# Modulation held as columns, small and expert loads moved ahead, and 29 instead of 31 fixed rounds in the second expert layer

## The reference, cut to what matters

```python
mod = silu(c) @ w_ada + b_ada                       # one row of 6 * 1024
sh1, sc1, g1, sh2, sc2, g2 = split(mod, 6)
h = rms_norm(x, norm1_g) * (1 + sc1) + sh1
ca, cb, q, k, v, gate_conv, gate_attn = split(h @ w_in)
merged = sigmoid(gate_conv) * conformer_conv(ca, cb) + sigmoid(gate_attn) * diff_attention(q, k, v)
x = x + g1 * (merged @ w_out)
h2 = rms_norm(x, norm2_g) * (1 + sc2) + sh2
x = x + g2 * (routed_experts(h2) + shared_expert(h2))
```

## Time and profile before

| | |
|---|---|
| median of 3 runs | 1488.78 us (1487.41 to 1489.77) |
| the profiled execution | 1488.66 us, span 1486.8 us |
| mean granted TensorE clock | 0.923 of full speed |
| TensorE (PE) | busy 1264.9 us, 85% |
| VectorE (DVE) | busy 543.6 us, 37% |
| ScalarE (ACT) | busy 278.4 us, 19% |
| DMA | 401.62 MB, mean 270 GB/s over the span |

### The profile page before, as it was taken

One profiled execution on the slowest core, in us unless ns is written; L12 is line 12 of the kernel. 1 busy time (PEld: TensorE's weight loads), 2 busy tenths in 40 slices (PEclk: granted clock), 3 DMA queues, 4 the chain that ended last, 5 costly groups with the idle time before them and its releaser, 6 DMA issues.

```text
span 1486.8 us, 23320 instructions
## 1 busy us (share of the span) xinstructions
PE 1264.9 (85%) x8581; PEld 679.5 (46%) x8581; DVE 543.6 (37%) x1598; ACT 278.4 (19%) x537; POOL 46.3 (3%) x131
## 2 busy tenths in 40 slices
PE   6998885679664668599998895899999999999996
PEld 4762243344322243484444442654454454454453
DVE  0003323343121121399974633443333333333334
ACT  2112321321000031201035310411111111111110
POOL 1001110200000000000000000300000000000000
PEclk9999777879887779799999997989999999999998
DMA  8557840378999958236300381659999999999994
GB/s 287 182 197 275 305 170 0 132 306 369 421 421 421 421 185 323 65 114 226 114 1 0 138 315 56 246 243 373 393 370 394 398 395 395 402 400 400 400 394 160
DMA packets 87906, 401.62 MB, mean 270 GB/s; under 512 B 10944, under 2 KB 19572, under 8 KB 59136
## 3 DMA queue, kind: packets, MB, share of 16 engines
q1 hardware_dynamic: 86608, 399.70, 68.7%
q10 hardware_dynamic: 816, 0.52, 0.2%
q0 software_dynamic: 384, 0.03, 0.0%
HBM read 399.15 MB, written 1.07 MB: 269 GB/s over the span
## 4 chain that ended last, share of the span: by engine, by line
PE 48%; DMA 4%; DVE 3%; ACT 2%; SPq 1%; issue 1%; DVEq 1%; ACTq 0%
PE ps L2083 14%; PE ps L401 13%; PE ps L429 7%; PE ps L365 5%; PE ps L374 3%; DMA big<-in_w_exp_down 3%; PE ps L2120 2%; PE ps L355 1%; PE ps L418 1%; PE ps L893 1%; SPq L1645 0%; DMA big<-mod 0%; DMA posi<-in_positions 0%; DVE big L1891 0%; DVE big L1889 0%
## 5 line engine op out<-in xcount | busy, mean ns | idle before, releaser
L401 PE MATMUL ps<-ring,big 128*32 128x512 f32 x2224 | 296.8, 618 | 57.2 <-DMA ring<-in_w_up 45.8
L401 PEld LDWEIGHTS ps<-ring,big 128*32 128x32 f32 x2224 | 86.0, 114 | 223.9 <-issue 223.8
L429 PE MATMUL ps<-big 128*32 128x512 f32 x1280 | 145.6, 595 | 12.6 <-DMA big<-in_w_exp_down 6.7
L2083 PE MATMUL ps<-ring,big 128*128 128x512 f32 x336 | 145.2, 593 | 3.2 <-DVEq L2065 1.6
L365 PEld LDWEIGHTS ps<-big 128*128 128x128 bf16 x2016 | 121.7, 99 | 34.5 <-issue 31.9
L401 PE MATMUL ps<-big 128*32 128x512 f32 x336 | 133.9, 616 | 3.3 <-DMA ring<-in_w_up 2.1
L365 PE MATMUL ps<-big 128*128 128x128 bf16 x2016 | 132.2, 222 | 1.4 <-ACT big L252 1.4
L1877 DVE SCALAR_TENSOR_TENSOR big<-big 128x256 f32<-128x256 f32 x240 | 105.6, 481 | 9.0
L2083 PEld LDWEIGHTS ps<-ring,big 128*128 128x128 f32 x336 | 63.6, 190 | 82.5 <-issue 78.4
L328 DVE TENSOR_TENSOR big<-big,ps 128x256 f32<-128x256 f32 x40 | 16.8, 421 | 225.1 <-ACT big L260 224.9
L374 PE MATMUL ps<-parts,slot_tok 128*128 128x512 f32 x320 | 86.6, 414 | 6.8 <-DVEq L347 6.8
(11 more groups left out here) (440 smaller groups left out, 1289.6 us busy)
## 6 DMA issues: line engine op xcount, KB each, us to landing
ring<-in_w_exp_gu SPq DMA_DIRECT2D x55, 2048.0 KB, 12.2
big<-in_w_exp_down SPq DMA_DIRECT2D x64, 1024.0 KB, 9.2
big<-in_w_down SPq DMA_DIRECT2D x32, 1024.0 KB, 18.3
ring<-in_w_in SPq DMA_DIRECT2D x15, 2048.0 KB, 7.9
ring<-in_w_gate SPq DMA_DIRECT2D x28, 1024.0 KB, 18.1
ring<-in_w_up SPq DMA_DIRECT2D x28, 1024.0 KB, 20.2
ring<-in_w_ada SPq DMA_DIRECT2D x12, 2048.0 KB, 8.0
big<-in_w_exp_gu SPq DMA_DIRECT2D x9, 2048.0 KB, 12.4
```

Of the source, the lines that this page charges most:

```text
L401: last = pe.matmul(ps[rows, BG, :], m.xsT[:, k, rows], m.gu(gu[j], k), start=(k == 0), stop=(k == KC - 1), skip_group_check=True)
L429: last = pe.matmul(ps[rows, BD + n, :], m.hidT[:, k, rows], m.dring[:, down[j], k * D + n * 512:k * D + n * 512 + 512], start=(k == 0), st ...
L2083: last = pe.matmul(bank, lhs(k), rhs(k), start=(k == 0 and start), stop=(k == kk - 1))
```

## The change

- `moe_sp`: the wait for the one-hot matrices goes. Down 2 and 3 are issued before `moe_sp`, down 1 after the last reader of `hT`, down 0 after the tokens' parts. GU 6 is issued before `moe_sp` too.
- First layer: GU 6 and down 2 and 3 follow GU 4 and 5. The small router tiles move out of the first columns of `work`.
- Second block: the last reader of `hT` is the shared expert's first product (`sh_gu`, 4), where it was its second (`sh_d`). Down 2 and 3 are issued once the merged branches are ready, GU 6 before GU 2 to 5. Router tiles and the shared expert's tiles move to memory that only the first block needed (`first_only`).
- Fixed rounds of the second layer: 29. Quad 1 and quad 13 have one where they had two.
- Modulation as columns: all vectors of the two norms are loaded as rows of 128, transposed at once, and VectorE makes `(1 + sc) * g` in 8 columns for each norm. VectorE scales the tokens by the inverse root alone; scale and shift are applied by ScalarE as it copies the transposed tokens out of PSUM. For the second norm VectorE also makes the token-major rows, after it has let TensorE go.
- The constants' loads (now 20, `w_in_c2`) are issued in the first block, after the loads of the gated projection and before the first loads for the second block. The rows of the second norm are issued after the last scores of the attention. The first norm's activation table is loaded before the barrier.

```diff
+def load_first_down(sp, m, ev, s):
+    sp.dma_start(m.dring[:, s, :], m.w_down[place(s):place(s) + 1].rearrange("o (p k) n -> p (o k n)", p=P)).then_inc(
+        ev(f"w_in_d{s}"), 16)
...
+    sp.wait_ge(ev(m.over[0]), m.over[1])
+    load_first_down(sp, m, ev, 1)
     sp.wait_ge(ev(m.p + "tok3"), 3 * TT)
-    sp.wait_ge(ev(m.over[0]), m.over[1])
-    sp.wait_ge(ev(m.p + "oneh"), 1)
-    for s in range(PER):
-        load_down(s)
-    load_gu(RING)
+    load_first_down(sp, m, ev, 0)
     sp.wait_ge(ev(m.p + "order"), 1)
...
-            m.over = ("sh_d", 1) if prefix == "b_" else ("router", 2)
+            m.over = ("sh_gu", 4) if prefix == "b_" else ("router", 2)
...
-        m2 = moe_buffers("b_", 64, [2, 2, 3] + [2] * 11 + [1] * 2, 48)
+        m2 = moe_buffers("b_", 64, [2, 1, 3] + [2] * 10 + [1] * 3, 48)
...
+        def modulated_out(act, name, done, gain, shift):
+            for c in range(KC):
+                act.wait_ge(ev(name), c // 2 + 1)
+                act.activation(hT[:, c, :], ps[:, 4 + c // 2, (c % 2) * T:(c % 2 + 1) * T], ACT.Identity,
+                               scale=mcols[:, gain + c:gain + c + 1], bias=mcols[:, shift + c:shift + c + 1])
+            act.drain().then_inc(ev(done), 1)
...
                 moe_sp_first(sp, m1, ev, PER, RING)
+                moe_sp_first(sp, m1, ev, RING, GU_SLOTS)
+                load_first_down(sp, m1, ev, 2)
+                load_first_down(sp, m1, ev, 3)
                 moe_sp(sp, m1, ev)
...
+                sp.wait_ge(ev("mod_out"), 16 * 12)
+                for j, v in enumerate((A["conv_dw_b_2"], A["conv_ln_g_2"], A["conv_ln_b_2"], A["norm1_g_2"],
+                                       mod[:, D:2 * D], mod[:, 0:D], A["norm2_g_2"], mod[:, 4 * D:5 * D],
+                                       mod[:, 3 * D:4 * D])):
+                    small(crows[KC * j:KC * j + KC, :], chunk_rows(v))
...
                 norm(act, "h4_ready", "rstd4")
+                act.preload_act_table_set(LOG_EXP)
...
                 sp.wait_ge(ev("at_s"), AH)
                 sp.dma_start(bcu[:, 0, :], vec(A["b_pw2_2"])).then_inc(ev("bcu_in"), 16)
                 sp.dma_start(bcu[:, 1, :], vec(mod[:, 2 * D:3 * D])).then_inc(ev("bcu_in"), 16)
-                for i in L_PW + L_O2 + [L_SGU, L_SD]:
-                    load(sp, i)
+                small(g2row[:], vec(A["norm2_g_2"]), "n4_in")
+                small(bc2[:, 0, :], vec(mod[:, 4 * D:5 * D]), "n4_in")
+                small(bc2[:, 1, :], vec(mod[:, 3 * D:4 * D]), "n4_in")
+                load(sp, L_SD)
                 moe_sp_first(sp, m2, ev, 0, 2)
-                sp.wait_ge(ev("h5_ready"), 1)
...
+                sp.wait_ge(ev("y2_ready"), 1)
                 small(rw2, A["w_router_2"][0].rearrange("(k p) n -> p k n", p=P), "rw2_in")
                 small(rb2, vec(A["router_bias_2"], 64), "rw2_in")
+                load_first_down(sp, m2, ev, 2)
+                load_first_down(sp, m2, ev, 3)
                 sp.wait_ge(ev("h6_ready"), 1)
                 sp.dma_start(g2row[:], vec(mod[:, 5 * D:6 * D])).then_inc(ev("g2_in"), 16)
+                moe_sp_first(sp, m2, ev, RING, GU_SLOTS)
                 moe_sp_first(sp, m2, ev, 2, RING)
...
-                chunks_out(act, "h6_T", "h6T_ready")
+                modulated_out(act, "h6_T", "h6T_ready", S2_SC, S2_SH)
+                act.wait_ge(ev("h6_ready"), 1)
                 part_out(act, m2, ev, 0)
...
-                dve.wait_ge(ev("n3_in"), 48)
-                modulated("rstd5", bcn[:, 0:D], bcn[:, D:2 * D], bcs)
+                dve.wait_ge(ev("dw_T"), 1)
+                dve.tensor_copy(cc, ps[:, 0, 256:256 + 3 * KC])
+                dve.tensor_copy(mcols[:, 0:6 * KC], ps[:, 0, 256 + 3 * KC:256 + 9 * KC])
+                dve.tensor_copy(dwc.rearrange("p c k -> p k c"), ps[:, 0, 0:248].rearrange("p (k c) -> p k c", c=KC))
+                dve.drain()
+                for g, sc in ((S_G, S_SC), (S2_G, S2_SC)):
+                    dve.scalar_tensor_tensor(mcols[:, sc:sc + KC], mcols[:, sc:sc + KC], 1.0, mcols[:, g:g + KC], ALU.add, ALU.mult)
+                dve.drain().then_inc(ev("mod_cols"), 1)
+                scale_rows(dve, "rstd5")
                 dve.drain().then_inc(ev("hn5_ready"), 1)
...
-                dve.wait_ge(ev("n4_in"), 48)
-                modulated("rstd6", bc2[:, 0, :], bc2[:, 1, :], bc2[:, 2, :])
+                scale_rows(dve, "rstd6", None, x_hat)
+                dve.drain().then_inc(ev("hn6_ready"), 1)
+                for t in range(TT):
+                    dve.tensor_tensor(hn_tm[:, t, :], x_hat[:, t, :], bc2[:, 0, :], ALU.mult)
+                dve.drain()
+                for t in range(TT):
+                    dve.tensor_tensor(hn_tm[:, t, :], hn_tm[:, t, :], bc2[:, 1, :], ALU.add)
                 dve.drain().then_inc(ev("h6_ready"), 1)
```

More of the change, by code:

```diff
@@ L596, in build_program @@
         ident = sb("ident", [P, P])
-        ntri = sb("ntri", [P, P])
-        nones = sb("nones", [P, P])
-        sel4 = sb("sel4", [MLH, MLH, P])
-        selq = sb("selq", [P, P])
-        rows = sb("rows", [N_ROWS, P])
+        first_only = sb("first_only", [P, 10 * P])
+        ntri, nones, selq = (first_only[:, P * j:P * j + P] for j in range(3))
+        rows = first_only[0:N_ROWS, 3 * P:4 * P]
+        sel4 = first_only[0:MLH, 4 * P:8 * P].rearrange("p (a b) -> p a b", a=MLH)
+        crep = first_only[:, 8 * P:10 * P].rearrange("p (a b) -> p a b", a=KC)
         cols = sb("cols", [P, N_ROWS])
```

127 lines of the change are left out of this document (57 added, 70 removed).

## The result

The changed kernel took 1471.26 us (median of 7 runs, 1468.47 to 1481.51) against 1489.11 (7 runs, 1484.81 to 1490.55): ratio 0.9894, 95% interval 0.9867 to 0.9921. Two later groups of runs on other chips gave 0.9851 (0.9824 to 0.9879) and 0.984 (0.9802 to 0.9879), medians 1470.03 and 1470.36 against 1491.43 and 1494.43. So it is faster, by 18 to 24 us, at 1470 to 1471 us. The forecast was 1463.3; some 7 to 8 us are to be found.

The account below looks back on a forecast made before the run. It took the first expert layer as DMA bound, the second block's mixers as compute bound, the second expert layer as TensorE bound by a hair. 8.7 + 8.7 + 1.5 + 6.5 = 25.4; 1488.66 - 25.4 = 1463.3 us, range 1454 to 1472.

Parts of the forecast that it names:

- Which stages are bound by what: First expert layer DMA bound, second block's mixers compute bound, second expert layer TensorE bound by a hair.
- Start of the second block, 8.7: First product at 606.5 instead of 615.20, gain 8.7 us; 0.2 taken for eight copies with scale and bias.
- Second norm, 8.7: Second block's second norm: TensorE starts at 918.1 instead of 927.28, casts come 8.7 us earlier, routing keeps its spacing.
- 17 to 18 were named as the sign: Second layer's first L401 product comes 17 to 18 us earlier than before, counted from the first layer's end.
- Early loads, 1.5 and 0: Both expert layers: DMA's idle time only moves behind these loads; gain 1.5 us in the first, nothing in the second.
- 29 rounds, 6.5: Second expert layer: two rounds of 15.83 us go, new waits follow; net 4.0 at quad 1, 2.5 at quad 13.
- The clock behind waits: Second expert layer, quads 2 and 15: GU product takes 9.80 us against 6.87 after each long wait, 2.9 lost.
- the first (loads eat both rounds): Rival, second expert layer: later landings turn the rounds' 6.5 us into 0 to 2; time 1469; chance 0.17.
- rounds not in full: Rival 2, expert layers: early loads fill the queue ahead and rounds count in full, 31.7 us; 1438; chance 0.03.
- the start not hidden: Rival 3, second block's start: gain hidden by first weights or VectorE's work, 8.7 us less; 1472; chance 0.07.
- the waits not smaller: Rival 4, expert layers: smaller waits, 12 us for the rounds and 3 in the first layer; 1456; chance 0.09.
- 38 activations by silu and so no extra round: Rival 5, second layer: extra rounds run behind quad 15, shown by over 38 silu activations; 1481 or 1499; chance 0.04.

Follow-up runs that it names:

- r30_q13: Changed kernel with quad 13's second round back in the second expert layer (30 rounds); 1471.62 us, against the changed kernel's 1470.03 on the same chip.
- norm_back: Changed kernel with the second norm's edit alone undone (broadcast rows, as before); 1485.2 us, ratio 0.995.
- fill_gaps: Changed kernel with idle matmuls where TensorE would stand, at the second block's start and the second norm, also behind the token transposes; 1467.67 us, ratio 0.9823.
- best: Changed kernel with fill_gaps' idle calls, ten each ahead of quads 2 and 15, and the extra-round loop cut from 48 to 8; 1462.83 us, ratio 0.9816.
- best2: Changed kernel with fill_gaps' idle calls, more ahead of quads 2 and 15 and the second layer's first row products, loop of 48 kept; 1460.88 us, ratio 0.9786.
- gaps_norm: Changed kernel with fill_gaps' idle matmuls at the second norm alone; 1467.53 us, ratio 0.9815.
- late_loads: Changed kernel without the early expert loads in both layers (GU 6 and down 0 to 3 behind the router's lists again); 1470.11 us, ratio 0.9851.
- after_b: The changed kernel itself, run again as the yardstick of a later group on its chip; 1470.36 us, ratio 0.984.
- fill_norm_start: Changed kernel with idle matmuls behind the second block's three small transposes and ahead of the second norm's scaled rows; 1470.71 us, ratio 0.986.

## Why the prediction was too low

- *Which stages are bound by what*: right. Nothing that the early loads did in the DMA-bound first layer came through; all that the start gained did.
- *Start of the second block, 8.7*: 8.1 came, the same in every kernel with this start but those with fillers. The root and the scalings were in time. The term that was mis-sized is the copies with scale and bias: 0.2 was taken for eight, it was 5.04 - 4.14 = 0.9. A single one takes 574 ns, where the plain copy takes 386; the trace of the kernel before even has eight copies out of PSUM with one operand from a column, 470 ns each (L872, 548.4 to 551.3), which I overlooked. The price was within my bounds; what failed is that waits for the transposes would hide it. The plain copies did wait for them, in pairs, 2.9 us for all eight; the new ones run without a wait and take 3.75. The Trainium skill has this ("ScalarE: Activation LUTs", section "What ACT_TABLE_LOAD costs"): each scale or bias taken from a column adds about 93 ns, by which the estimate for 256 columns is 186 + 2 x 93 + 213 = 585; the 574 ns of the row agree to 2%. What the step left out is TensorE's clock. Before, the first product started with it at 1.00; now TensorE has stood 9.4 and 3.6 us beforehand, and the clock is 0.50 until 3.3 to 4.4 us into the product. From that product to TensorE's last ahead of the norm it is 298.5 to 299.1 in three traces of the changed kernel, 297.8 in r30_q13 and norm_back, where the clock came back earlier, and 297.0 before. That is 1.5 to 2 us, and the clock is a part of it: in the kernels where it was at 1.00 from the first product on (r30_q13, norm_back, fill_gaps, best, best2) the stretch took 296.9 to 298.1.
- *Second norm, 8.7*: this is the step that failed, and it failed behind the point up to which I had worked it out. The sum put TensorE's clock behind the shorter gap at nothing; it cost 3 to 5 us, and of the 8.7 there came 5.7, 6.3 and 6.3 up to the first GU product in the three traces (58.2 us before, 52.5, 51.9 and 51.9 now). Transposes, casts and the wait put ahead of them are as forecast (idle 15.13 to 5.92; casts 8.7 earlier, counted from the moment when `h5` is there). The prediction then let everything behind move along. The products of router and shared expert did not: at a clock of 0.50 they took 3 to 5 us longer than before, and TensorE became what the shared hidden rows waited for. fill_gaps and gaps_norm show the clock as the cause: with the gaps filled the products take 3.79 and 14.03 us again, and the whole stretch is 49.3 us, so that 8.9 come where 8.7 were forecast. Counted from the barrier the first GU product came 12.2 us earlier (360.5 us after it, 372.7 before), where 17 to 18 were named as the sign. norm_back shows the edit's worth only from above, since it is itself slower here than the kernel before (64.8 against 58.2).
- *Early loads, 1.5 and 0*: nothing in both (late_loads). The mechanism (the idle time only moves) is right; of the 1.5 that I let through nothing came: waits for GU weights fell by 2.3, those for down weights rose by 1.7.
- *29 rounds, 6.5*: right in sum, 5 to 6.4 by the traces, wrong in its parts: 5.4 for quad 1 (4.0 forecast), 0 for quad 13 (2.5 forecast). That the sum is right is partly luck, for the two errors cancel in part. For quad 13 I set one round against 25.0 + 2.5 us of loads; the run without it says that the end was already the last load's. At quad 2 the wait and the slow product were as written down.
- *The tail*: no term was there for it. 2.6 to 2.7 us between the last down product and the last combine; its cause is open.
- *The clock behind waits*: I charged 2.9 us behind each of the two long waits and nothing behind idle times that became shorter. The 2.9 took 9.80 from the timeline and 6.87 from the chain of waits, which count differently (in one view it is 2.75), and the 9.80 was the slowest of five such products (8.48 to 9.80). Measured it is 2.0 and 1.9. The lesson is that a shorter gap did not bring a shorter stretch at the low clock: 17 us of it before and after.
- Of the rivals, the first (loads eat both rounds) has its symptom only at quad 13. The second to fifth are excluded: rounds not in full, the start not hidden, the waits not smaller, 38 activations by silu and so no extra round.

In sum, 25.4 forecast against 20.2: -0.6 at the start, -1.5 in the mixers behind it, +0.5 of idle time and -5.0 + 1.5 of what follows at the norm, -1.7 in the first layer, -0.6 in the rounds and tail together (up to the last down product 8.4 were gained, of which 2.7 are the first GU product, 9.72 before and 7.07 in this execution; the wait at the tail took back 2.7), and +2.2 for the untouched first stages, which differ between executions of the same kernel as well (first expert product at 310.2, 311.0 and 310.3 in three traces of the changed kernel, at 307.4 to 317.4 over all).

## What to carry over

Where an edit shortens a wait of TensorE, work on to the end of the products behind it and ask at which granted clock they will run: a gap that shrinks from 15 to 6 us can leave as much low clock as before, and then it lies under the products instead of in the idle time. Cheap idle matmuls in such gaps, up to the last of them, are a test of this; here, in all the gaps together (best2), they were also a gain. In a layer whose rounds take hardly longer than its loads (31.66 against 30.0 us a quad here), price a removed round by the load that comes last and not by its own length.

## What the chip showed

- The clock fell again within the router's product where TensorE had stood 1.5 us (after_b) or 2.6 us (fill_norm_start) ahead of it, and stayed at 1.00 where it had stood 0.84 (fill_gaps, gaps_norm). The same kernel came back to full clock at different points in different executions (16 us after the norm's transposes began in the first trace; in after_b at first after 3, then for good after 13).
- One stretch can flip with it: the first GU product of the second layer took 7.07 us in the changed kernel's first trace and 9.52 in after_b's, the same instructions.
- Ten idle calls (20 matmuls of 512 columns in the records) take 8.85 us, which is how the fillers were sized.
- In the second layer DMA moved 392 and 398 GB/s from 1060 to 1100 and from 1100 to 1400 us with TensorE busy throughout, at a DMA share of 0.97 and 0.99, and 435 and 421 in the two waits (1006.5 to 1017, 1420 to 1430), at 1.02 and 0.99. But it also moved 425 from 985 to 1000 and 437 from 1032 to 1038, with TensorE busy 14.68 of 15 and 5.91 of 6 us: that TensorE's work slows the loads is not shown.
